# State read-out in four column groups, masked values in two row groups (HGRN sample products)

## The chip, the cores and the metric

The kernel runs on one core of a Trainium2 chip. The metric is the device time of one execution in microseconds; three runs of the kernel before gave a median of 1787.67 us (1786.09 to 1790.24). The profile is of one execution of it. Its engines are named as in the profile: PE (TensorE; PEld are its weight loads), DVE (VectorE), ACT (ScalarE), POOL (GpSimd) and SP, whose queue issues most of the DMAs.

## The reference

One decoder layer is run on 256 prompt tokens and on 32 sample tokens (8 sequences of 4). A conditioning projection (ada), one combined input projection, two mixing groups, an output projection, layer norms and a mixture of 32 experts follow each other. The change is in the first mixing group, a gated linear recurrence with 8 heads of 128 x 128 state:

```
S_t = diag(f_t) S_{t-1} + k_t v_t^T          # per head, state S of 128 x 128
o_t = S_t^T q_t
```

The reference computes it by chunks; for the samples a chunk is the 4 new tokens of a sequence:

```python
o_inter = jnp.einsum('bhtk,bhkv->bhtv', qc * jnp.exp(b), S)      # read-out of the old state
a = jnp.einsum('bhtk,bhsk,bhtsk->bhts', qc, kc, decay)
o_intra = jnp.einsum('bhts,bhsv->bhtv', a, vc)
S_new = jnp.exp(b_last)[..., None] * S + jnp.einsum(
    'bhsk,bhsv->bhkv', kc * jnp.exp(b_last[:, :, None] - b), vc)
```

Each of the 8 sample sequences has its own state per head, so per head there are 8 products of 4 tokens with a 128 x 128 state (`o_inter`), and 8 updates of 128 x 128 (`S_new`). Everything is float32.

## The kernel before

Each engine has one instruction stream written out by hand; semaphores order them. Tokens stand as columns: 256 of the prompt (`TP`) and 32 of the samples (`TS`), 288 in all (`T`). Weights arrive as 1 MB chunks in a ring of 8 slots (`ring`); SP loads the next chunk into a slot when PE has signalled `ring_used` for it. The order of PE's stream is: ada chunks and the projections of the recurrent group, then two *halves* of four heads each (L672 to L746), then the attention group, the output projection, routing and the experts.

In a half, PE alternates between dense work and the recurrence. A dense chunk (`head_chunk`, L589) is 16 matmuls of 128 x 128 weights by 288 columns, for the attention's q and k. Behind each even chunk come eight small products for the prompt's state (L708), with 32 rows each in two of the four row groups of the array and two PSUM banks. Behind each odd chunk comes one sample head:

- L718: the read-out. `qpad` holds, for each sequence b, the head's 32 query columns with all but the four of sequence b zeroed. Eight matmuls (128 rows, 32 columns, 128 moving columns) accumulate over b into the 32 partitions `32h` of bank 3, so the four heads of a half stand below one another.
- L720: the product inside the 4 new tokens (32 rows, 32 columns) is accumulated onto it, and signals `os_pe`.
- L726: the update. POOL (L497) has made `vblk`, the 32 tokens' values repeated for 8 sequences and masked with `seqmask`: 32 partitions x 1024. Two matmuls of 32 rows, 128 columns and 512 moving columns write banks 0 and 1. DVE scales the old state (L1625, after `os_pe`) and adds both banks (L1630); POOL stores the new state and loads that of the head after next.

At the start of a half PE transposes the decayed keys of its four heads: the prompt's (L686) and the samples' (L689, four transposes into 32 partitions of bank 7), which ACT copies out (L1220, L1221). At its end stand the prompt's output products (L740 and L745, the latter with 32 moving columns), and between their two pairs of heads one transpose (L734) of `osr`, DVE's copy (L1635) of the four read-outs; DVE copies the transposed result to its place (L1637). PE then waits for ACT's copy of the first pair (L1227). A whole group's value rows are projected before, with 4 partial sums for the samples that `fold_parts` (L613) adds by a matmul with `fold`, four stacked 32 x 32 identities; ACT and DVE each copy half of the 1024 columns to `tok[0:32, 5]` (L1179, L1512).

Every plain fp32 matmul shows as two records in the trace, a transpose as one.

## Time and profile before

| | |
|---|---|
| median of three runs | 1787.67 us |
| profiled execution, device time | 1787.84 us |
| its span, first to last instruction | 1786.1 us |
| PE busy | 1603.4 us (90%) |
| DVE, ACT, POOL busy | 528.3, 200.0, 94.7 us |
| mean granted TensorE clock | 0.945 |

The granted clock is given as a share of 2.4 GHz; in a stretch it reads 1.00 or 0.50. A record's duration includes its way through the array, so records of one engine overlap, and busy time is the union of them. An idle time before an instruction is given in brackets with what ended it; "issue" means that nothing the profile shows was waited for. Forms such as 128*32 are the rows and columns of the weights that a matmul uses, and 128x512 the shape that moves through them.

### The profile page before, as it was taken

The numbers are of one execution on the slowest core, as the hardware profiler recorded it, in microseconds if no ns is written. First come the engines' busy times: TensorE is split into PE (matmuls) and PEld (weight loads), VectorE is DVE, ScalarE is ACT, GpSimd is POOL, SyncE is SP. The second block draws the span as 40 slices with busy tenths as digits, with TensorE's granted clock in tenths as the row PEclk, the third lists the DMA queues.
The fourth block names the chain that finished last, engine by engine and source line by source line (L and its number), as shares of the span: only waits on it lengthen the run. The fifth ranks groups of instructions, "written<-read, shape, count | busy, mean of one in ns | idle before, by whom it ended". The sixth has DMA issues, their size and how long they took to land.

```text
span 1786.1 us, 24827 instructions
## 1 busy us (share of the span) xinstructions
PE 1603.4 (90%) x9535; PEld 913.9 (51%) x9535; DVE 528.3 (30%) x919; ACT 200.0 (11%) x335; POOL 94.7 (5%) x172
## 2 busy tenths in 40 slices
PE   3679999999999999899967999999898988999893
PEld 0036666634777775477744544454443534445351
DVE  0010009631221322542145223232323223232225
ACT  0000001300000002340025000101000000000002
POOL 3000000000110100000001000000000000000000
PEclk7679999999989989899987999999999999999997
DMA  9998888876443445184332999999999999999991
GB/s 350 422 386 333 308 333 306 328 289 237 159 129 97 151 142 186 49 314 142 141 141 107 363 407 415 401 421 421 409 411 404 412 399 411 407 414 414 414 393 61
DMA packets 79389, 536.94 MB, mean 301 GB/s; under 512 B 10385, under 2 KB 10561, under 8 KB 18065
## 3 DMA queue, kind: packets, MB, share of 16 engines
q1 hardware_dynamic: 72146, 507.62, 71.6%
q0 software_dynamic: 6576, 26.35, 4.8%
q10 hardware_dynamic: 624, 2.36, 0.3%
q8 instruction: 31, 0.51, 0.1%
q14 instruction: 12, 0.10, 0.0%
HBM read 533.40 MB, written 11.80 MB: 305 GB/s over the span
## 4 chain that ended last, share of the span: by engine, by line
PE 69%; DMA 19%; DVE 5%; SPq 4%; issue 2%; ACT 2%; ACTq 0%; DVEq 0%
PE ps L589 18%; PE ps L1095 13%; DMA ring<-w_gate 12%; PE ps L933 7%; PE ps L602 6%; PE ps L1115 5%; DMA ring<-w_ada 5%; PE ps L573 4%; SPq L383 3%; PE ps L1077 3%; DMA arena<-w_down 1%; PE ps L1041 1%; PE ps L745 1%; DVE arena L1917 1%; PE ps L1083 1%
## 5 line engine op out<-in xcount | busy, mean ns | idle before, releaser
L1095 PE MATMUL ps<-ring,arena 128*64 128x256 f32 x3200 | 359.4, 383 | 17.9 <-DMA ring<-w_gate 17.9
L589 PE MATMUL ps<-arena,ring 128*128 128x288 f32 x1280 | 321.7, 410 | 0.0
L1095 PEld LDWEIGHTS ps<-ring,arena 128*64 128x64 f32 x3200 | 227.2, 138 | 165.4 <-DMA ring<-w_gate 33.7
L589 PEld LDWEIGHTS ps<-arena,ring 128*128 128x128 f32 x1280 | 240.6, 190 | 89.8 <-issue 25.5
L1115 PE MATMUL ps<-arena 128*64 128x512 f32 x800 | 180.6, 597 | 29.7 <-DMA arena<-w_down 16.7
L573 PE MATMUL ps<-ring,silu_c 128*32 128x512 f32 x768 | 118.3, 727 | 51.2 <-DMA ring<-w_ada 24.6
L1115 PEld LDWEIGHTS ps<-arena 128*64 128x64 f32 x800 | 53.8, 136 | 140.4 <-issue 86.5
L933 PE MATMUL ps<-arena,ring 128*128 128x288 f32 x512 | 124.7, 406 | 0.0
L602 PE MATMUL ps<-ring,arena 128*128 128x512 f32 x256 | 117.2, 606 | 1.3 <-ACT arena L1179 0.7
L1077 PE MATMUL ps<-arena 64*128 64x512 f32 x384 | 104.6, 636 | 12.2 <-DVE arena L1917 10.7
L933 PEld LDWEIGHTS ps<-arena,ring 128*128 128x128 f32 x512 | 97.2, 190 | 26.8
L1933 DVE TENSOR_TENSOR arena<-arena,ps 128x256 f32<-128x256 f32 x25 | 10.5, 421 | 276.9 <-PE ps L1095 276.9
L573 PEld LDWEIGHTS ps<-ring,silu_c 128*32 128x32 f32 x768 | 20.6, 118 | 128.8 <-DMA ring<-w_ada 68.6
L602 PEld LDWEIGHTS ps<-ring,arena 128*128 128x128 f32 x256 | 47.5, 193 | 61.3 <-issue 58.1
L1077 PEld LDWEIGHTS ps<-arena 64*128 64x128 f32 x384 | 31.0, 184 | 86.8 <-issue 86.8
L1946 DVE TENSOR_TENSOR arena<-ps,arena 128x512 f32<-128x512 f32 x25 | 17.3, 691 | 164.6 <-PE ps L1115 164.6
L1917 DVE TENSOR_TENSOR arena<-arena,ps 128x1024 f32<-128x1024 f32 x48 | 58.6, 1221 | 11.3 <-PE ps L1077 8.5
L539 POOL DMA_INDIRECT arena<-u_rows,idx x26 | 29.9, 1152 | 534.3 <-PE ps L1041 533.3
L1367 ACT COPY arena<-ps 128x1024 f32<-128x1024 f32 x26 | 26.3, 1012 | 198.8 <-PE ps L1041 198.8
L1374 ACT ACTIVATE arena<-ps 128x256 f32<-128x256 f32 x25 | 9.6, 384 | 314.6 <-PE ps L1095 314.6
L1496 DVE COPY arena<-ps 128x288 f32 x8 | 3.7, 458 | 132.0 <-PE ps L589 132.0
L497 POOL TENSOR_TENSOR arena<-arena,seqmask 32x1024 f32<-32x1024 f32 x8 | 15.2, 1905 | 414.8 <-DVE arena L1512 414.7
(432 smaller groups left out, 1214.7 us busy)
## 6 DMA issues: line engine op xcount, KB each, us to landing
ring<-w_gate SPq DMA_DIRECT2D x100, 1024.0 KB, 23.9
ring<-w_up SPq DMA_DIRECT2D x100, 1024.0 KB, 26.3
arena<-w_down SPq DMA_DIRECT2D x100, 1024.0 KB, 27.0
ring<-w_ada SPq DMA_DIRECT2D x96, 1024.0 KB, 8.3
ring<-w_in SPq DMA_DIRECT2D x56, 1024.0 KB, 6.4
ring<-w_o SPq DMA_DIRECT2D x16, 1024.0 KB, 6.5
ring<-cache_k SPq DMA_DIRECT2D x16, 512.0 KB, 3.9
ring<-cache_v SPq DMA_DIRECT2D x16, 512.0 KB, 4.0
```

Source lines behind the costliest of these rows:

```text
L383: sp.dma_start(dst, src).then_inc(signal, 16)
L539: nc.gpsimd.indirect_dma_start(out=xg, out_offset=None, in_=u2_rows[:], in_offset=bass.IndirectOffsetOnAxis(idx1[:, 0:1], 0), bounds_check ...
L573: last = mm(ps[32 * j:32 * j + 32, 0, :], silu_c[:, t, :], ring[:, slot, 512 * j:512 * (j + 1)], start=(t == 0), stop=(t == KC - 1))
L589: last = mm(ps[:, bank, 0:T], ring[:, slot, P * t:P * (t + 1)], uT[:, t, :], start=(t == 0), stop=(t == KC - 1))
L602: mm(ps[:, 4 + i, :], uT[:, 4 * (c % 4) + t, t0:t0 + tn], ring[:, slot, 512 * t:512 * (t + 1)], start=(c % 4 == 0 and t == 0), stop=(c % 4 ...
L745: last = mm(o[:, CH * c4:CH * (c4 + 1)], shist[:, c - 1, h, :], hq[:, k, CH * c:CH * (c + 1)], start=False, stop=(c4 == 3))
L933: last = mm(ps[:, 4 + m % 4, 0:T], ring[:, n % SLOTS, P * k:P * (k + 1)], mixT[:, k, :], start=(k == 0), stop=(k == KC - 1))
L1077: last = mm(ps[0:tn, ((5, 6), (4, 7))[nn][r], :], spread[rows, t0:t0 + tn], yg[rows, 512 * nn:512 * (nn + 1)], start=True, stop=True, tile ...
L1095: last = mm(ps[B * s:B * (s + 1), 2 + c // 4, 0:256], xgT[:, 4 * (c % 4) + t, :], ring[:, c, 512 * t + 256 * s:512 * t + 256 * (s + 1)], s ...
L1115: last = mm(ps[B * s:B * (s + 1), 5 + nn, :], hT[:, q % 2, B * (q // 2):B * (q // 2 + 1)], mslot[q][:, 1024 * s + 512 * nn:1024 * s + 512 ...
L1367: nc.scalar.copy(xgT, ps[:, 0:2, :].rearrange("p a (m s) -> p (a m) s", s=B)).then_inc(x_copied, 1)
L1917: return v.tensor_tensor(w, w, ps[:, 5:7, :], ALU.add).then_inc(sum_dve, 1)
```

## The change

- **Read-out.** The eight matmuls of a head go to four column groups: sequence `2j + i` writes the partitions `32j`, `i` = 0, 1 accumulate there, and each head has 128 columns of bank 3 instead of 32 partitions. The product inside the new tokens is accumulated in group 0. The four partial sums are added when the result is turned: DVE copies all of bank 3 (128 x 512, into `bg2`) and four matmuls with `fold` turn and add it, in place of one transpose.
- **Masked values.** The values, the decayed keys and the mask are held twice, on partitions 0 to 31 for sequences 0 to 3 and on 32 to 63 for 4 to 7. `vblk` becomes 64 x 512, and the two matmuls of the update use row groups 0 and 1 and write banks 0 and 1. PE waits once, for all adds of the head before, and not for each bank.
- For the second copy, `fold_parts` runs twice, the four transposes of the sample keys become eight matmuls with the identity into two column groups, and ACT and DVE copy 64 partitions for 32. POOL makes `seqsel` with two small copies before it lets PE start.

```diff
+            for j in range(2):
+                link(g.tensor_copy(seqsel[32 * j:32 * j + 32, :], seqmask[:, 4 * j:4 * j + 4]))
...
-                nc.gpsimd.tensor_tensor(vblk, bc(tok[0:TS, 5, h * P:(h + 1) * P], 1, NSEQ),
-                                        bc(seqmask[:], 2, P), ALU.mult).then_inc(vblk_ready, 1)
+                nc.gpsimd.tensor_tensor(vblk, bc(tok[0:2 * TS, 5, h * P:(h + 1) * P], 1, 4),
+                                        bc(seqsel[:], 2, P), ALU.mult).then_inc(vblk_ready, 1)
...
-            def fold_parts(parts):
+            def fold_parts(parts, copies=1):
-                mm(ps[0:TS, 6, :], fold[:], parts, start=True, stop=True).then_inc(folded, 1)
+                for j in range(copies):
+                    last = mm(ps[32 * j:32 * j + 32, 6, :], fold[:], parts, start=True, stop=True)
+                last.then_inc(folded, 1)
...
                 for h in range(4):
-                    last = nc.tensor.transpose(ps[0:TS, 7, P * h:P * (h + 1)], hf[:, heads[h], TP:T], ident[:])
+                    for j in range(2):
+                        last = mm(ps[32 * j:32 * j + 32, 7, P * h:P * (h + 1)], hf[:, heads[h], TP:T], ident[:],
+                                  start=True, stop=True)
...
-                    for b in range(NSEQ):
-                        mm(ps[32 * h:32 * h + 32, 3, 0:P], qpad[:, h, b, :], s0[k % 2][:, b, :],
-                           start=(b == 0), stop=False)
-                    mm(ps[32 * h:32 * h + 32, 3, 0:P], abufs[:, k, :], tok[0:TS, 5, P * k:P * (k + 1)],
+                    for i in range(2):
+                        for j in range(4):
+                            mm(ps[32 * j:32 * j + 32, 3, P * h:P * (h + 1)], qpad[:, h, 2 * j + i, :],
+                               s0[k % 2][:, 2 * j + i, :], start=(i == 0), stop=(i == 1 and j > 0))
+                    mm(ps[0:TS, 3, P * h:P * (h + 1)], abufs[:, k, :], tok[0:TS, 5, P * k:P * (k + 1)],
                        start=False, stop=True).then_inc(os_pe, 1)
                     pe.wait_ge(vblk_ready, k + 1)
-                    for part in range(2):
-                        if k >= 1:
-                            pe.wait_ge(us_dve, 3 * k - 1 + part)
-                        mm(ps[:, part, :], kdts[:, h, :],
-                           vblk[:, 4 * part:4 * part + 4, :].rearrange("p b v -> p (b v)"), start=True, stop=True
-                           ).then_inc(us_pe, 1)
+                    if k >= 1:
+                        pe.wait_ge(us_dve, 3 * k)
+                    for j in range(2):
+                        mm(ps[:, j, :], kdts[32 * j:32 * j + 32, h, :],
+                           vblk[32 * j:32 * j + 32].rearrange("p b v -> p (b v)"), start=True, stop=True,
+                           tile_position=(32 * j, 0)).then_inc(us_pe, 1)
...
-                        nc.tensor.transpose(ps[:, 3, P:2 * P], osr, ident[:]).then_inc(osr_pe, 1)
+                        for h in range(4):
+                            last = mm(ps[:, 3, TS * h:TS * (h + 1)], osr[:, P * h:P * (h + 1)], fold[:],
+                                      start=True, stop=True)
+                        last.then_inc(osr_pe, 1)
...
-                v.tensor_copy(osr, ps[:, 3, 0:P]).then_inc(osr_dve, 1)
+                v.tensor_copy(osr, ps[:, 3, :]).then_inc(osr_dve, 1)
```

PE's stream keeps its order. From the last chunk of the first half to the end of its sample head it read (names in brackets are the semaphores waited for):

```order
L589 MATMUL ps<-arena,ring 128x288 x15
L718 MATMUL ps<-arena 32x128 [waits s0_loaded1]
L718 MATMUL ps<-arena 32x128 x7
L720 MATMUL ps<-arena 32x128
L726 MATMUL ps<-arena 128x512 [waits us_dve,vblk_ready]
L726 MATMUL ps<-arena 128x512 [waits us_dve]
```

Now it reads, with the projection as L592, the read-out L726, the product inside the tokens L728 and the update L734:

```order
L592 MATMUL ps<-arena,ring 128x288 x15
L726 MATMUL ps<-arena 32x128 [waits s0_loaded1]
L726 MATMUL ps<-arena 32x128 x7
L728 MATMUL ps<-arena 32x128
L734 MATMUL ps<-arena 128x512 [waits us_dve,vblk_ready]
L734 MATMUL ps<-arena 128x512
```

The counts are the same; one wait is gone, and the groups of the array that the matmuls use (which don't show here) differ. From the middle of the first half's output products to the first chunk of the second half PE's stream was:

```order
L745 MATMUL ps<-arena 128x32 x4
L734 MATMUL ps<-ident,arena 128x128 [waits osr_dve]
L740 MATMUL ps<-arena 128x128 [waits hgo_act]
L745 MATMUL ps<-arena 128x32 x3
...
L686 MATMUL ps<-ident,arena 128x128 x7
L689 MATMUL ps<-ident,arena 32x128 x4
L589 MATMUL ps<-arena,ring 128x288 [waits evac_act,slot_loaded0]
```

and is now (output products L751 and L756, fold L743, prompt transposes L691, sample keys L695):

```order
L756 MATMUL ps<-arena 128x32 x4
L743 MATMUL ps<-fold,bg 128x32 [waits osr_dve]
L743 MATMUL ps<-fold,bg 128x32 x3
L751 MATMUL ps<-arena 128x128 [waits hgo_act]
L756 MATMUL ps<-arena 128x32 x3
...
L691 MATMUL ps<-ident,arena 128x128 x7
L695 MATMUL ps<-ident,arena 32x128 x8
L592 MATMUL ps<-arena,ring 128x288 [waits evac_act,slot_loaded0]
```

One transpose has become four matmuls ahead of the wait for ACT, and four transposes eight matmuls ahead of the first chunk.

## Rows read from the trace of the kernel before

**Rows 1.** The page: busy tenths of PE in 40 slices of the span.

```profile
PE   3679999999999999899967999999898988999893
```

**Rows 2.** Stretches: PE, PEld, DVE, ACT, POOL busy (instructions), PEclk, DMA share, GB/s.

```profile
436.00:523.40 87.40, 87.40 (x437) 64.61 (x436) 24.39 (x41) 3.07 (x6) 13.75 (x11) 1.00 0.43 140
523.50:540.50 17.00, 15.82 (x71) 14.90 (x71) 0.91 (x9) 1.87 (x3) 3.60 (x4) 0.50 0.30 78
540.60:625.80 85.20, 85.20 (x420) 62.57 (x418) 22.04 (x32) 2.27 (x6) 10.30 (x8) 1.00 0.39 130
625.90:642.90 17.00, 16.59 (x79) 16.20 (x79) 1.51 (x2) 1.17 (x2) 1.64 (x3) 0.50 0.16 47
```

**Rows 3.** Waits of SP's queue, 430 to 1000 us: total us, times, longest.

```profile
SPq L335 <- PE ps L589: 102.3, 11, 11.5
SPq L394 <- DVE plan L1875: 10.9, 1, 10.9
```

**Rows 4.** Timeline, first sample head, PE: start us, us, what [idle before].

```profile
454.09 1.94 PE L718 MATMUL ps<-arena 128*32 128x128 f32 x16
455.95 0.40 PE L720 MATMUL ps<-arena 32*32 32x128 f32 x2
456.28 1.98 PE L726 MATMUL ps<-arena 32*128 32x512 f32 x4
458.19 8.03 PE L589 MATMUL ps<-arena,ring 128*128 128x288 f32 x32
```

**Rows 5.** Timeline: rotating column groups (L809), alternating row groups (L708, L1077).

```profile
759.39 1.93 PE L809 MATMUL ps<-ring,arena 128*32 128x128 f32 x64
...
445.04 1.16 PE L708 MATMUL ps<-arena 32*128 32x128 f32 x16
...
1378.33 2.10 PE L1077 MATMUL ps<-arena 64*128 64x512 f32 x8
```

**Rows 6.** Timeline: transposes of the sample keys, first and second half.

```profile
436.75 0.60 PE L689 MATMUL ps<-ident,arena 128*32 128x128 f32 x4
...
538.70 1.06 PE L689 MATMUL ps<-ident,arena 128*32 128x128 f32 x4
```

**Rows 7.** Timeline: the second value fold and DVE's copies around it.

```profile
433.25 0.69 DVE L1508 COPY arena<-ps 128x512 f32<-128x512 f32 x1 [7.37 <-PE ps L607]
434.00 1.05 PE L613 MATMUL ps<-arena,fold 128*32 128x512 f32 x2 [0.81 <-DVE arena L1508]
435.08 0.68 DVE L1512 COPY arena<-ps 32x512 f32<-32x512 f32 x1
```

**Rows 8.** Timeline: end of the first half, around the read-out's transpose.

```profile
522.25 0.28 DVE L1635 COPY arena<-ps 128x128 f32<-128x128 f32 x1
...
525.88 1.75 PE L745 MATMUL ps<-arena 128*128 128x32 f32 x8
527.45 0.45 PE L734 MATMUL ps<-ident,arena 128*128 128x128 f32 x1
527.67 0.58 ACT L1227 COPY arena<-ps 128x512 f32<-128x512 f32 x1 [18.80 <-PE ps L745]
528.31 0.80 PE L740 MATMUL ps<-arena 128*128 128x128 f32 x2 [0.41 <-ACT arena L1227]
```

**Rows 9.** Timeline: start of the program on POOL and PE.

```profile
15.83 0.93 POOL L478 COPY fold<-ident 32x32 f32<-32x32 f32 x4
18.91 4.40 PE L573 MATMUL ps<-ring,silu_c 128*32 128x512 f32 x24 [18.91 <-POOLq L486]
22.25 0.16 PEld L573 LDWEIGHTS ps<-ring,silu_c 128*32 128x32 f32 x8 [1.43 <-DMA ring<-w_ada]
```

**Rows 10.** Timeline of the key transposes after the halves; stretches around them.

```profile
639.32 4.58 PE L759 MATMUL ps<-ident,arena 128*128 128x128 f32 x24
639.20:642.90 3.70, 3.70 (x19) 3.61 (x19) 1.22 (x1) 0.59 (x1) 0.01 (x1) 0.50 0.00 0
643.00:646.00 3.00, 3.00 (x14) 1.73 (x13) 2.34 (x2) 0.00 (x0) 1.34 (x3) 1.00 0.57 228
```

More of the change, by code:

```diff
@@ L76, in layer @@
         fold = sb("fold", [P, TS])
+        seqsel = sb("seqsel", [2 * TS, 4])
         silu_c = sb("silu_c", [P, KC, 32])
@@ L148, in layer @@
         shist = area(TMP, 8, 4, P)
-        kdts = area(TMP + 4096, 4, P, parts=TS)
+        kdts = area(TMP + 4096, 4, P, parts=2 * TS)
         abuf = area(TMP + 4608, 2, H, P)
@@ L154, in layer @@
         kdt = area(TMP + 7040, 2, 4, P)
-        osr = area(TMP + 8064, P)
-        vblk = area(TMP + 8192, NSEQ, P, parts=TS)
+        osr = bg2[:]
+        vblk = area(TMP + 8192, 4, P, parts=2 * TS)
         s0 = [area(TOK + 1024 * i, NSEQ, P) for i in range(2)]
@@ L657, in _ @@
                     pe.wait_ge(parts_act, 1)
-                    fold_parts(parts_hi)
+                    fold_parts(parts_hi, 2)
                     pe.wait_ge(evac_act, 15)
@@ L671, in _ @@
             pe.wait_ge(parts_dve, 1)
-            fold_parts(parts_hi)
+            fold_parts(parts_hi, 2)
             pe.wait_ge(evac_dve, 15)
@@ L1178, in evacuate_rows @@
                 act.wait_ge(folded, n_fold)
-                nc.scalar.copy(tok[0:TS, slot + 2, 0:512], ps[0:TS, 6, :]).then_inc(evac_act, 1)
+                nc.scalar.copy(tok[0:2 * TS, slot + 2, 0:512], ps[0:2 * TS, 6, :]).then_inc(evac_act, 1)
             act.wait_ge(lb_dve, 1)
@@ L1220, in _ @@
                 nc.scalar.copy(kdt, ps[:, 0:2, :].rearrange("p a (h s) -> p a h s", s=P))
-                nc.scalar.copy(kdts, ps[0:TS, 7, :].rearrange("p (h s) -> p h s", s=P)).then_inc(kd_act, 1)
+                nc.scalar.copy(kdts, ps[0:2 * TS, 7, :].rearrange("p (h s) -> p h s", s=P)).then_inc(kd_act, 1)
                 for c in range(0, SLOTS, 2):
@@ L1511, in evacuate_rows @@
                 dve.wait_ge(folded, n_fold)
-                v.tensor_copy(tok[0:TS, slot + 2, 512:1024], ps[0:TS, 6, :]).then_inc(evac_dve, 1)
+                v.tensor_copy(tok[0:2 * TS, slot + 2, 512:1024], ps[0:2 * TS, 6, :]).then_inc(evac_dve, 1)
             N_G = N_MIX + 2 * MIX + 2
@@ L1634, in _ @@
                     dve.wait_ge(osr_pe, 1)
-                v.tensor_copy(osr, ps[:, 3, 0:P]).then_inc(osr_dve, 1)
+                v.tensor_copy(osr, ps[:, 3, :]).then_inc(osr_dve, 1)
                 dve.wait_ge(osr_pe, half + 1)
-                v.tensor_copy(hout[:, heads, TP:T], ps[:, 3, P:2 * P].rearrange("p (h t) -> p h t", t=TS)
+                v.tensor_copy(hout[:, heads, TP:T], ps[:, 3, 0:P].rearrange("p (h t) -> p h t", t=TS)
                               ).then_inc(osm_dve, 1)
```

## The prediction

> **What bounds the kernel now.** I read the slices of the span first: PE reads 8 or 9 tenths in most slices [rows 1]. The change touches one stage, the recurrent head group from about 436 to 643 us, so the stretches of that stage come next [rows 2]. From 436 to 523.4 us PE is busy 87.40 of 87.40 us at a granted clock of 1.00 (the 2.4 GHz level) with the DMA engines at 0.43. From 523.5 to 540.5 and from 625.9 to 642.9 us the clock reads 0.50 (1.2 GHz) and PE is still busy 15.82 and 16.59 of 17 us. So PE's own stream sets the pace here, at either level. The waits of the DMA queue say the same from the other side: SP waited 102.3 us in total for PE to free ring slots before it could load more w_in [rows 3], so weights lie ready.
>
> A microsecond taken from PE in this stage should therefore arrive at the end of the span if nothing later is pinned to an absolute time. The expert loads are the only place where DMA bounds later, and SP waited 10.9 us there for the routing plan [rows 3], which comes out of the PE, DVE and ACT chain. The loads start earlier when the plan does.
>
> Inside the stage the timeline of one sample head [rows 4] shows what stands between two dense projection chunks: 16 records of the state read-out (each fp32 matmul is two records) in 1.94 us, two of the intra-sample product, then four records of the masked-value product in 1.98 us. From the first read-out record at 454.09 to the next chunk at 458.19 are 4.10 us, eight times in all.
>
> **Read-out in four column groups.** Now all 16 records of a head write the same 32 partitions, one after the other: a record lasts 0.27 us, so the step is (1.94 - 0.27) / 15 = 0.111 us. The value product of the attention later has the same shape (128 rows by 32 columns, 128 moving columns) and rotates over four column groups: 64 records in 1.93 us [rows 5], so one round of four takes the step of one record here. Sixteen records in four rounds take 0.27 + 3 x 0.111 = 0.60 us. Saved: 1.94 - 0.60 = 1.34 us a head, 10.7 us over eight heads. Ends: 0 if nothing overlaps, 10.7 if all does. I take 10.7, as the row has the same shape and the same rotation.
>
> **Masked values in two row groups.** The four records step at (1.98 - 0.59) / 3 = 0.46 us. Two row groups with a bank each exist already: the prompt's state update runs 16 records of 32 rows in 1.16 us where the 16 of the read-out need 1.94, and the expert combine runs 8 records of 64 rows by 512 columns in 2.10 us [rows 5]. By the first, a pair takes 0.06 x 2 = 0.12 us against 0.111 for one; by the second, a round of two steps (2.10 - 0.64) / 3 = 0.49 us. Two rounds: 0.61 + 0.49 = 1.10 us. Saved 0.88 us a head, 7.0 us over eight (ends: 0 and 7.3, the latter with a step of 0.46). The two separate waits of before become one on the adds of the previous head, two dense chunks back; behind it in PE's queue stands the next chunk, and the adds wait for nothing but PE. GpSimd's masking instruction has half the elements a partition, so the state stores queued behind it don't get later.
>
> **The doubled transposes.** Four transposes a half (one record each) become eight matmuls against the identity (16 records) in two column groups: eight rounds for four. At the high level a step is (0.60 - 0.27) / 3 = 0.11 us, at the low one (1.06 - 0.42) / 3 = 0.21 us [rows 6], and the second half starts at the low level. Added: 4 x 0.11 + 4 x 0.21 = 1.3 us on PE's path (ends: 0 at no extra rounds, 3.8 if the groups don't overlap and twelve records are added). ACT's copy of 64 instead of 32 partitions is the same length: DVE's 32x512 copy takes 0.68 us, its 128x512 copy 0.69 [rows 7].
>
> **The fold products.** One transpose a half becomes four matmuls, 8 records of 128 by 128 weights with 32 moving columns, the shape of the inter-chunk product before it: 8 records in 1.75 us at the low level [rows 8], that is 0.21 each, 1.7 us to the next start. Now PE goes from the transpose (527.45) to the next product (528.31) in 0.86 us, of which most is the wait for ACT's copy [rows 8]. So 0.84 us comes on the path a half, 1.7 in all (ends: about 0 at the high level, where ACT's copy hides it, and 1.7).
>
> In front of it DVE copies 128x512 where it copied 128x128: 0.69 for 0.28 us [rows 7, 8]. The copy starts at 522.25, PE wants it at 527.45: hidden by 5 us of products, and 0.41 us a half if that cover were gone. The Trainium skill (TensorEngine Tiling (Array Packing), PSUM Bottleneck) warns that tiling speeds up the matmuls and not the emptying of PSUM, so that the copy can become the bound. By that rule the copy would cost up to 0.8 us over both halves; the rows leave 4.5 us of slack and I take 0.
>
> **The two value folds of the projection** run twice into two column groups. Two records take 1.05 us [rows 7]; two more in another group run beside them, 0 taken, 0.9 us over both calls if they don't.
>
> **Two small mask copies** are added on GpSimd before it lets PE start. Four such copies take 0.93 us [rows 9], two 0.5. PE starts at 18.91 behind GpSimd but is out of loaded weights at 22.25 [rows 9], so the delay is swallowed: 0, or 0.5 us.
>
> **Sum:** -10.7 - 7.0 + 1.3 + 1.7 = -14.7 us. The profiled execution took 1787.84 us (span 1786.1 and 1.7 around it), 0.2 above the median of 1787.67. 1787.84 - 14.7 = 1773.1 us.
>
> **The clock.** Both low stretches begin shortly after PE reaches the narrow products at the end of a half and end after the transposes that follow. At half level PE takes twice as long per step (0.21 for 0.11), so a low stretch longer or shorter by x us moves the end by x / 2. The new blocks are shorter and denser, the fold products are more of the narrow kind; I take no net effect and keep 4 us either way, which is also the spread of the three runs (1786.09 to 1790.24). The Trainium skill (TensorE: Matmul & The Clock Gate, Part 4) says that PE transposes don't count as activity for the clock. By that rule the identity matmuls that replace transposes would bring the second half back to the high level sooner, at most 0.9 us. The trace speaks against it: from 639.2 to 642.9 PE does nothing but transposes at 0.50, and reads 1.00 from 643.0 on [rows 10]. I take 0.
>
> **Rivals.**
> Overlap of neighbours only. Both records of a matmul go to the same column group one behind the other; if PE starts them strictly in order, the second record of one overlaps only the first of the next. The read-out would take 9 steps for 16 (0.78 us saved), the masked product 3 for 4 (0.46): 9.9 us saved, the transposes would cost 1.6, the folds 1.7 and 0.9, in all -5.7: 1782. Against it: 64 records in 1.93 us are four abreast [rows 5].
> Column groups only. The masked product signals after each of its two matmuls, and the rows of two groups in [rows 5] may signal once. If that holds the pair apart, 7.0 us are not won: 1780. For it there is no row; against it, two matmuls into two banks share nothing.
> Given back later. A later stage is set by a transfer and swallows the gain: 1787.5. Against it the waits of SP [rows 3].
> Slower. The sparser activity between chunks drops the clock inside a half, over dense chunks. A stretch of 17 us at 0.50 costs up to 8.5 us of dense work. It decides from 1.7 such stretches on; with two the kernel takes 1773.1 + 17 = 1790. Against it: before, the eight blocks were twice as long, and within the halves the clock read 1.00 throughout [rows 2].
>
> **Chances.** Forecast 80%, neighbours only 7%, column groups only 5%, given back 4%, slower 4%. A difference of 0.2% (3.6 us) is about what can be told from none. Below 1784.1 lie the first three: 92%, of which I move 2 to no change for the terms not bounded by a row. Faster 0.90, same 0.05, slower 0.05. The range goes down by the fold at the high level (1.7) and some 3.4 us of clock to 1768, and up to 1781.5, which takes in the second rival and ends half a microsecond short of the first.
>
> **What would show it.** In the changed profile: a read-out of 16 records in about 0.60 us and a masked product in about 1.1 us, so 2.0 us less between chunks eight times; 16 identity records in about 0.9 and 1.7 us; 8 fold records of 1.7 us a half with no wait for DVE; two low stretches of about 17 us at the ends of the halves and none inside; the routing plan and the first expert block some 14 us earlier. The prediction is wrong if a read-out block takes 1 us or more, if the clock reads 0.50 inside a half, or if the plan comes earlier and the end doesn't.

## The result and the profile after

The changed kernel took 1752.23, 1757.92 and 1760.06 us, the middle one the median (one further run of 6512 us was disturbed and counts in nothing here), the kernel before 1786.09 to 1790.24 us beside it. The ratio is 0.9824, with an interval of [0.9808, 0.9839]: some 31 us faster, about twice the 14.7 us of the forecast, and below the range that ended at 1768.0. The profiled execution of it is the fastest, 1752.23 us (span 1750.5). A later comparison gave 1757.63 us (1755.13 to 1761.97, five runs) and 0.9827 [0.9809, 0.9845].

PE stays the busiest engine; the slices of the page answer to [rows 1], the same view before the change:

```profile
PE   3679999999999999899967999999989989889893
```

The stretches of the recurrent stage answer to [rows 2], cut where the granted clock changes (us, PE, PEld, DVE, ACT, POOL busy with instructions, PEclk, DMA share, GB/s):

```profile
435.00:512.90 77.90, 77.90 (x433) 56.83 (x433) 20.79 (x38) 3.08 (x6) 9.63 (x10) 1.00 0.41 146
512.90:518.40 5.50, 5.50 (x52) 5.50 (x50) 3.31 (x8) 0.58 (x1) 0.93 (x1) 1.00 0.65 265
518.40:532.00 13.60, 12.84 (x62) 11.28 (x62) 0.53 (x7) 2.07 (x3) 2.69 (x3) 0.50 0.20 59
532.00:606.70 74.70, 74.70 (x405) 54.23 (x404) 19.15 (x29) 1.59 (x4) 7.73 (x8) 1.00 0.41 136
606.70:622.40 15.70, 15.19 (x114) 12.93 (x113) 6.80 (x8) 1.17 (x2) 3.29 (x5) 1.00 0.44 179
```

The reader is to see two things. The heads before the first output product take 77.90 us for some 85.7. And of the two low stretches of 17 us one has become 13.6 us and begins 5.5 us behind the first output product; the other, at the end of the second half, is gone in this profile.

The first sample head on PE answers to [rows 4] (read-out, product inside the tokens, masked product, next chunk):

```profile
454.02 0.64 PE L726 MATMUL ps<-arena 128*32 128x128 f32 x16
454.59 0.40 PE L728 MATMUL ps<-arena 32*32 32x128 f32 x2
454.92 1.13 PE L734 MATMUL ps<-arena 32*128 32x512 f32 x4
455.98 0.75 PE L592 MATMUL ps<-arena,ring 128*128 128x288 f32 x2
```

From 454.02 to 455.98 are 1.96 us where 4.10 stood. The doubled keys of both halves answer to [rows 6]:

```profile
436.02 1.07 PE L695 MATMUL ps<-ident,arena 128*32 128x128 f32 x16
...
527.83 1.92 PE L695 MATMUL ps<-ident,arena 128*32 128x128 f32 x16
```

The second value fold and DVE's copy of it answer to [rows 7]; four records take the 1.05 us that two took:

```profile
433.16 1.05 PE L617 MATMUL ps<-arena,fold 128*32 128x512 f32 x4 [0.81 <-DVE arena L1519]
434.26 0.68 DVE L1523 COPY arena<-ps 64x512 f32<-64x512 f32 x1
```

The end of the second half, at the high level, answers to [rows 8]: DVE's copy of the read-out, the last products of the first pair, the fold products, ACT's copy, the second pair.

```profile
609.06 0.68 DVE L1646 COPY bg<-ps 128x512 f32<-128x512 f32 x1
...
609.92 0.98 PE L756 MATMUL ps<-arena 128*128 128x32 f32 x8
...
610.73 1.06 PE L743 MATMUL ps<-fold,bg 128*128 128x32 f32 x8
610.93 0.58 ACT L1238 COPY arena<-ps 128x512 f32<-128x512 f32 x1 [14.75 <-PE ps L756]
611.60 0.30 PEld L751 LDWEIGHTS ps<-arena 128*128 128x128 f32 x2
611.62 0.47 PE L751 MATMUL ps<-arena 128*128 128x128 f32 x2
```

The fold products run without a wait, and 0.89 us after their start the second pair starts; before it was 0.86 from the transpose to there. In the first half they stand at the high level too, from 516.92 to 517.82 us. SP's waits answer to [rows 3], the mask copies and PE's start to [rows 9], the key transposes behind the halves, at the high level in this profile, to [rows 10]:

```profile
SPq L336 <- PE ps L592: 94.5, 11, 11.4
...
SPq L395 <- DVE plan L1886: 10.7, 1, 10.7
```

```profile
15.83 0.42 POOL L478 COPY seqsel<-seqmask 32x4 f32<-32x4 f32 x2
16.31 0.93 POOL L481 COPY fold<-ident 32x32 f32<-32x32 f32 x4
...
19.39 3.64 PE L576 MATMUL ps<-ring,silu_c 128*32 128x512 f32 x16 [19.39 <-POOLq L489]
...
615.65 1.94 PE L770 MATMUL ps<-ident,arena 128*128 128x128 f32 x16
```

To see where the rest came from I cut every profile at the same instructions: *heads* from the first key transpose to the first output product, and in the second half from its first dense chunk; *ends* from the first output product to the next half's first chunk or the attention's first transposes of cached keys; *experts* from the first expert product to the first product behind the last block. All in us, from one profiled execution each; "fall" is the time from the first output product to the fall of the granted clock to 0.50, first half / second half.

| kernel | heads | ends | of it at 0.50 | fall | experts |
|---|---|---|---|---|---|
| before | 170.5 | 40.8 | 33.1 | 2.0 / 1.5 | 772.3 |
| before, again | 171.5 | 41.6 | 34.7 | 1.2 / 2.4 | 773.5 |
| after | 154.9 | 32.5 | 11.3 | 5.5 / none | 766.7 |
| after, again | 154.2 | 33.0 | 12.7 | 10.5 / 6.5 | 765.9 |
| x1 read-out only | 160.8 | 27.5 | 1.2 | 10.6 / none | 774.2 |
| x2 masked values only | 164.0 | 32.9 | 13.6 | 7.3 / 7.2 | 764.9 |
| x3 before + added work | 171.5 | 44.0 | 36.5 | 1.3 / 1.5 | 774.3 |
| x4 after + dense filler | 169.5 | 36.4 | 20.5 | 5.8 / 4.8 | 765.9 |
| x5 before + dense at the ends | 175.6 | 32.4 | 14.2 | 6.8 / 7.2 | 773.6 |
| x6 after + 8 narrow products | 157.5 | 27.6 | 0 | none / none | 765.1 |
| y2 after + a copy of the old block | 161.8 | 39.0 | 26.3 | 6.6 / 2.8 | 769.3 |

Before to after, the two first profiles: heads -15.6, ends -8.3, experts -5.6; the attention's score and value products 50.2 to 45.2, -5.0; all other stages -1.1; together -35.6, the difference of the spans. The -5.0 is an accident of the execution: both programs show 48.4 there in their second profile, where the rest is heads -17.3, ends -8.6, experts -7.6. So three things have to be explained: the work of the heads (forecast), the ends of the halves, and the experts, which the change doesn't touch.

### The profile page after: what moved, and what is told of

It reads as the page before. It is cut to its first block, busy times and chain, and to the rows that moved or that the text cites. A ratio compares the mean times of both kernels' runs of the same rounds, so it can differ in the third digit from the quotient of the medians.

```text
span 1750.5 us, 24913 instructions
## 1 busy us (share of the span) xinstructions
PE 1570.4 (90%) x9577; PEld 891.4 (51%) x9577; DVE 527.8 (30%) x919; ACT 200.1 (11%) x335; POOL 88.2 (5%) x174
## 4 chain that ended last, share of the span: by engine, by line
PE 68%; DMA 18%; DVE 5%; SPq 4%; issue 2%; ACT 2%; ACTq 0%; DVEq 0%
PE ps L592 18%; DMA ring<-w_gate 14%; PE ps L1106 13%; PE ps L944 7%; PE ps L605 6%; PE ps L1126 6%; DMA ring<-w_ada 5%; PE ps L576 4%; SPq L384 3%; PE ps L1088 3%; PE ps L1052 1%; DVE arena L1928 1%; PE ps L796 1%; PE ps L610 1%; PE ps L1094 1%
## 5 line engine op out<-in xcount | busy, mean ns | idle before, releaser
L592 PE MATMUL ps<-arena,ring 128*128 128x288 f32 x1280 | 322.2, 411 | 0.0
L592 PEld LDWEIGHTS ps<-arena,ring 128*128 128x128 f32 x1280 | 241.1, 191 | 89.6 <-issue 25.6
L1088 PE MATMUL ps<-arena 64*128 64x512 f32 x384 | 104.6, 636 | 12.3 <-DVE arena L1928 10.7
L1944 DVE TENSOR_TENSOR arena<-arena,ps 128x256 f32<-128x256 f32 x25 | 10.5, 421 | 277.4 <-PE ps L1106 277.4
L1957 DVE TENSOR_TENSOR arena<-ps,arena 128x512 f32<-128x512 f32 x25 | 17.3, 692 | 158.4 <-PE ps L1126 158.4
L1928 DVE TENSOR_TENSOR arena<-arena,ps 128x1024 f32<-128x1024 f32 x48 | 58.6, 1221 | 11.3 <-PE ps L1088 8.5
L1378 ACT COPY arena<-ps 128x1024 f32<-128x1024 f32 x26 | 26.3, 1012 | 198.3 <-PE ps L1052 198.3
L1388 ACT COPY arena<-ps 128x512 f32<-128x512 f32 x25 | 14.6, 585 | 188.2 <-PE ps L1126 188.2
```

The source lines that it names most:

```text
L592: last = mm(ps[:, bank, 0:T], ring[:, slot, P * t:P * (t + 1)], uT[:, t, :], start=(t == 0), stop=(t == KC - 1))
L1088: last = mm(ps[0:tn, ((5, 6), (4, 7))[nn][r], :], spread[rows, t0:t0 + tn], yg[rows, 512 * nn:512 * (nn + 1)], start=True, stop=True, tile ...
L1378: nc.scalar.copy(xgT, ps[:, 0:2, :].rearrange("p a (m s) -> p (a m) s", s=B)).then_inc(x_copied, 1)
L1928: return v.tensor_tensor(w, w, ps[:, 5:7, :], ALU.add).then_inc(sum_dve, 1)
```

## The experiments

### Which part gives what

**x1**, the kernel before with the read-out in four column groups and its fold products alone, shown here; **x2**, the masked values, keys and mask on two row groups alone (the change with x1's edit undone).

```diff
- mm(ps[32 * h:32 * h + 32, 3, 0:P], qpad[:, h, b, :], s0[k % 2][:, b, :],
+ mm(ps[32 * j:32 * j + 32, 3, P * h:P * (h + 1)], qpad[:, h, 2 * j + i, :],
...
- nc.tensor.transpose(ps[:, 3, P:2 * P], osr, ident[:]).then_inc(osr_pe, 1)
+ last = mm(ps[:, 3, TS * h:TS * (h + 1)], osr[:, P * h:P * (h + 1)], fold[:],
```

> The kernel before with the read-out in four column groups and the fold product alone; masked values and sample keys as before. The changed kernel gained some 30 us where the work on TensorE explains 15; the rest is less time at the low clock (the second half's low stretch is gone, that of the attention is shorter). By work alone: read-out -8 x 1.3 = -10.4, fold 0 to +1.7, so 9 to 10.5 us under the kernel before. Theory A, sparse activity (the narrow blocks pull the clock down at the ends of the halves, and fewer narrow records pull less): 9 to 10.5 and at least 5 more from the clock, 15 or more under it. Theory B, chance (where a low stretch falls is an accident of each program): 10 give or take 4, the runs' clocks scattering about that of before. Theory C, matmuls in place of transposes hold the clock up: like A, with the clock gain at the second half's end, since the fold is here.

> The kernel before with the masked values in two row groups alone (with the doubled sample keys and value folds); read-out and its transpose as before. By work alone: -8 x 0.86 = -6.9, doubled transposes +0.4 to +1.3: 5.6 to 6.5 us under the kernel before. Theory A (sparse activity): that and some 3 to 8 us from the clock. Theory B (chance): 6 give or take 4. Theory C (matmuls for transposes): a gain of clock at the starts of the halves, where the identity matmuls are.

x1: 1770.21 us (1762.33 to 1778.95), 0.9911 [0.9886, 0.9936]. x2: 1768.35 us (1765.86 to 1771.84), 0.9896 [0.9882, 0.9911]. Alone, the parts win 17.6 and some 19 us, together more than the 31 of both. The table says why: heads -9.7 and -6.5 add up to about the change's, but the profiles show that each part alone already takes the early fall of the clock away, which can be won once. x1 fits theory A (15 us or more) and theory C as well, which x3 tests. x2 won more than A had for it (8.6 to 14.5 us): its experts are short too, x1's are not. Six runs of x1 lie in two groups, 1762 to 1765 us at a mean clock of 0.955 to 0.957 and 1775 to 1779 us at 0.949 to 0.951. The profile is of the first group; that the second had longer low stretches is what the mean clock suggests, and no profile shows where.

x1's ends: 10.6 us at 1.00 behind the first output product, then 3.4 at 0.50, and the second end wholly at 1.00.

```profile
516.80:527.40 10.60, 9.83 (x88) 9.73 (x88) 3.03 (x13) 1.17 (x2) 4.48 (x4) 1.00 0.55 167
527.40:530.80 3.40, 3.40 (x13) 2.57 (x12) 0.00 (x0) 1.48 (x2) 0.00 (x0) 0.50 0.24 78
608.90:624.60 15.70, 15.19 (x113) 12.94 (x113) 5.95 (x8) 1.17 (x2) 3.29 (x5) 1.00 0.45 158
```

### Does the added work hold the clock up?

**x3**, the kernel before with the identity matmuls in place of the sample key transposes and narrow products in place of the read-out's transpose, no more.

```diff
- last = nc.tensor.transpose(ps[0:TS, 7, P*h:P*(h+1)], hf[:, heads[h], TP:T], ident[:])
+ for j in range(2): last = mm(ps[32*j:32*j+32, 7, P*h:P*(h+1)], hf[:, heads[h], TP:T], ident[:], ...)
```

> The kernel before with only the change's added matmuls: eight identity matmuls for four transposes of the sample keys, four narrow matmuls for the transpose of the read-out; read-out and update as slow as before. By work: +1.3 for the sample keys, 0 to +1.7 for the narrow ones: 1 to 3 us over the kernel before. Theories A and B: that, with low stretches at the ends of both halves as before. Theory C (matmuls where transposes were hold the clock up): 5 us or more under the kernel before, the second half's low stretch gone.

1790.76 us (1777.92 to 1796.64, twelve runs), 0.9996 [0.9971, 1.002]. In its profile the early falls are all there, at 1.3 and 1.5 us. Inconclusive all the same: four of the twelve runs took 1778 to 1780 us at a mean clock of 0.958 to 0.959, the other eight 1786 to 1797 us at 0.945 to 0.950, and no profile shows what was different in the four. This work may help in some executions; it doesn't do what the change does in all of them.

### What stands between the heads and the output products

**x4**, the change with four dense products (128 x 128 by 288 columns, result unused) behind each masked product; **x5**, the kernel before with the same four behind the last head of each half only; **x6**, the change with eight narrow products (32 columns out, unused) there.

```diff
+ for t in range(4): mm(ps[:, 7, 0:T], ident[:], uT[:, t, :], ...)             # x4, x5
...
+ for t in range(8): mm(ps[0:TS, 7, 0:P], uT[:, t, TP:T], ident[:], ...)       # x6
```

> The changed kernel with four dense matmuls (128 x 128 weights, 288 columns, results unused) behind each sample head, 8 records of 0.243 us, some 2.1 us with their drain, so that a head takes about as long as before, 17 us in all. Theory A (sparse activity): the clock gain stays, 17 us over the changed kernel, about 1775, no low stretch at the second half's end. If it is the length of a head, or the moment at which the ends of the halves fall, that decides: the low stretches are back and the time is that of the kernel before, 1788 to 1790. Theory B (chance): anything between 1775 and 1792, by where the stretches fall.

> The kernel before with four dense matmuls (128 x 128 weights, 288 columns, results unused) only behind the last sample head of each half, in front of the output products: some 2.1 us twice, 4.2 us of added work. Theory A (the sparse head in front of the narrow output products pulls the clock down early, 1.5 to 2.0 us after the first of them in the profile before): the clock falls later at the ends of both halves, the low stretches there are shorter than 17 us, and the kernel is no slower than before: 1780 to 1788. Theory B (chance) and theory C (matmuls for transposes): the stretches at the ends stay at about 17 us, 1787.8 + 4.2 = 1792.

> The changed kernel with eight matmuls into one column group (128 rows, 32 columns, 128 moving columns, results unused) only behind the last sample head of each half: 16 records in 1.94 us as the read-out of before, 3.9 us of added work. Theory A: the clock falls early again at the ends of both halves, within 2 to 3 us of the first output product, and stays low for some 14 to 17 us: 1757.9 + 3.9 + 5 to 12 = 1767 to 1774. Theories B and C: 1757.9 + 3.9 = 1762, stretches as in the changed kernel.

x4: 1776.23 us (1766.02 to 1777.96), 0.9925 [0.9905, 0.9945]. The time is the one forecast with theory A, but its profile has a low stretch at the second half's end, which A there had excluded: the falls come at 5.8 and 4.8 us, and 20.5 us are at 0.50. With heads about as long as before (169.5 us) the fall stays late, so the pace of the heads alone doesn't bring it early. What stands right ahead of the output products is dense work here, as in x5. x5: 1785.64 us (1781.97 to 1787.13), 0.9979 [0.9969, 0.9989]: 2.0 us of dense work at each end put the fall off to 6.8 and 7.2 us and shorten the ends from 40.8 to 32.4 us, which pays for the 4 to 5 us longer heads and leaves some 3 us:

```profile
524.10:530.90 6.80, 6.27 (x56) 6.08 (x55) 2.52 (x9) 0.58 (x1) 3.48 (x3) 1.00 0.54 131
530.90:541.20 10.30, 9.53 (x39) 8.32 (x39) 0.12 (x1) 2.06 (x3) 0.09 (x1) 0.50 0.13 42
626.10:633.30 7.20, 6.67 (x60) 6.48 (x58) 0.29 (x1) 0.58 (x1) 1.09 (x2) 1.00 0.39 112
```

x6: 1760.83 us (1752.42 to 1765.32), 0.9847 [0.983, 0.9864], no fall in its profile. Theory A had forecast an early fall and 1767 to 1774 us, and missed: 1.9 us of narrow work behind the fast block isn't enough to bring the early fall back.

**y2** therefore put all of the old block there: eight narrow products and two masked products over 32 rows, results unused, behind the last head of each half; the signal of that head's update to DVE moves behind them.

```diff
+ for t in range(8): mm(ps[0:TS, 7, 0:P], uT[:, t, TP:T], ident[:], ...)
+ for j in range(2): mm(ps[:, 7, :], kdts[0:TS, h, :], vblk[0:TS]..., ...).then_inc(us_pe, 1)
```

> The changed kernel with a copy of the old head block behind the last head of each half: 8 products into 32 columns and 2 products over 32 rows with 512 columns moving, results unused, some 3.7 us each time. Theory A (4 us of work on a part of the array right before the output products bring the early fall of the clock): the clock falls within 2.5 us of the first output product at both ends, the ends measure 18 to 20 and 21 to 23 us without the copy's own 3.7 us, and the time is 1758 + 7.4 + 8 = 1773 us. Rival (the copy's place alone, without what surrounded it before, does nothing to the clock): no fall within 4.8 us of it, time 1758 + 7.4 = 1765 us.

1773.72 us (1768.04 to 1776.41), 0.9923 [0.9905, 0.9941], the time of theory A, but the early fall in one half only. The block takes its 3.8 us; the fall comes 2.8 us behind the first output product in the second half, and 6.6 us in the first. Some 3 us of the time are of another kind: the experts take 769.3 us, with 13.2 us of idle time on PE for which the profile shows no wait, where x4 has 9.9. So the hit of the time is partly luck. The lines are the block, and the stretches around both first output products (517.93 and 613.9):

```profile
514.16 1.94 PE L741 MATMUL ps<-ident,arena 128*32 128x128 f32 x16
516.02 1.98 PE L743 MATMUL ps<-arena 32*128 32x512 f32 x4
517.93 0.49 PE L759 MATMUL ps<-arena 128*128 128x128 f32 x2
```

```profile
517.90:524.50 6.60, 6.60 (x60) 6.57 (x59) 2.72 (x8) 0.59 (x1) 2.63 (x4) 1.00 0.26 83
524.50:534.80 10.30, 9.53 (x49) 8.29 (x49) 1.19 (x5) 1.56 (x3) 0.99 (x1) 0.50 0.25 74
613.90:616.70 2.80, 2.80 (x27) 2.80 (x26) 1.29 (x2) 0.00 (x0) 1.39 (x2) 1.00 0.00 0
616.70:633.80 17.10, 17.10 (x82) 16.56 (x82) 2.74 (x3) 1.17 (x2) 1.02 (x3) 0.50 0.16 65
```

What is shown: with the old block of 4.1 us right ahead of the output products the clock fell within 3 us in both halves of all nine profiles that have it (the two of before, x3 and the six below that only move memory); without it, or with dense work between, not before 4.8 us, or not at all, in 16 ends (the change twice, x1, x2, x4 to x6, and x8 below); with the old block put behind the new one, in one of two. x5 adds nothing to the kernel before but dense work at that place, and puts the fall off. What of the block the chip answers to was not told apart.

### The two kernels again

> The changed kernel itself, once more, for a second profile and more times. If the clock's stretches belong to the program (A, C): again a short or no low stretch at the second half's end, median 1755 to 1762. If they are accidents of a run (B): stretches at the ends of halves of any length, times scattered from 1752 up to 1773, where the work alone would put it.

> The kernel before itself, for a second profile. A and C: low stretches of some 17 us at the ends of both halves again, beginning within 3 us of the first output product. B: other places or lengths; the stage of the experts, which the change doesn't touch, shows what differs between two profiles of one program.

1757.63 us for the change and 1788.39 us for one run of before: the second profiles of the table. The experts' difference stays, the attention's doesn't. At the ends the change has 12.7 us at 0.50 for 11.3, but in other places: 3.4 us in the first half and, against theory A's letter, 10.2 us in the second, where the first profile had none. What the change keeps is the late fall, not a half without one.

### Why the experts got faster

The programs whose experts take some 766 us are those that hold `seqsel` (after, x2, x4, x6; y2 holds it too, and takes 3 us more for the idle time named there). Its 16 bytes per partition take up 32 behind `fold`, and every later tensor lies 32 bytes higher: the arena, into which `w_down` is loaded, at byte 101888 instead of 101856. **x7** is the kernel before with an unused tensor of the same size; **x8** the change with `seqsel` declared behind the arena.

```diff
         fold = sb("fold", [P, TS])
+        pad = sb("pad", [2 * TS, 4])            # x7, from before
-        seqsel = sb("seqsel", [2 * TS, 4])      # x8, from after
...
         arena = sb("arena", [P, ARENA])
+        seqsel = sb("seqsel", [2 * TS, 4])      # x8
```

> The kernel before with one unused tensor of 32 bytes per partition put behind `fold`, where the change has `seqsel`; no instruction differs, but every later tensor of the on-chip memory lies 32 bytes higher, the arena at byte 101888 instead of 101856. Theory L (the 7 to 8 us of the stage of experts come from where the tensors lie): the stage falls from some 773.5 to some 766 us and the time to 1780 to 1781 us; the ends of the halves stay at 39 to 43 us. Rival M (they come from the different work in the attention before it, by the clock or by the order of the transfers): stage 773 to 774 us, time 1788 us as before.

> The changed kernel with `seqsel` declared behind the arena, so that the arena and all before it lie where they lay in the kernel before; the instructions are those of the change. Theory L: the stage of experts is back at some 773.5 us and the time 7 to 8 us over the changed kernel's, 1765 to 1767 us. Rival M: stage 766 us, time 1757 to 1759 us.

x7: 1781.91 us (1779.02 to 1782.61), 0.9962 [0.9949, 0.9974], experts 766.6 us, ends 40.1. x8: 1764.84 us (1758.64 to 1767.28), 0.9869 [0.985, 0.9889], experts 773.4 us. Both as the theory of the layout has it. What is shorter on PE is a wait. The line is the down projection, its busy time, the mean of one and the idle time ahead of it with what ended it, of the kernel before and of x7, whose instructions are the same:

```profile
L1115 PE MATMUL ps<-arena 128*64 128x512 f32 x800 | 180.6, 597 | 29.7 <-DMA arena<-w_down 16.7 <-DVE arena L1935 12.9
```

```profile
L1116 PE MATMUL ps<-arena 128*64 128x512 f32 x800 | 180.2, 597 | 22.0 <-DVE arena L1936 12.9 <-DMA arena<-w_down 9.1
```

And the loads themselves run faster. The lines are what the DMA engines moved from 980 to 1700 us, of the kernel before and of x7, whose first expert products start at 988.8 and 988.7 us. x7 moved 0.75% more in the same time; 0.75% of 772 us are, as an estimate, 5.8 us, for the 5.6 that its experts are shorter:

```profile
DMA packets 41532, 292.86 MB, mean 407 GB/s; under 512 B 5851, under 2 KB 5851, under 8 KB 5979
```

```profile
DMA packets 41835, 295.07 MB, mean 410 GB/s; under 512 B 5885, under 2 KB 5885, under 8 KB 6013
```

**x11** moves the arena alone, by 32 bytes; **x9** and **x10** move everything behind `fold` by 96 and 64; **x12** and **x13** the arena alone by 160 and 288. All are the kernel before with one pad, as x7's, behind `fold` or ahead of the arena.

> The kernel before with a pad of 32 bytes directly ahead of the arena: the arena at byte 101888, every other tensor of the attention where it was. Theory D (what counts is where the transfers into the arena land, above all `w_down`): as the pad behind `fold`, stage of experts some 766.6 us, time 1780 to 1782 us. Rival (another tensor's place counts): 773 us and 1787 us.

> The kernel before with a pad of 96 bytes behind `fold`: the arena at byte 101952, a multiple of 64 and not of 128 or more. Theory D with a boundary of 64 bytes: time 1780 to 1782 us, stage of experts some 766.6 us. If a coarser boundary (128 or 512 bytes) counts: 1787 us, stage 773 us.

> The kernel before with a pad of 64 bytes behind `fold`: the arena at byte 101920, 32 bytes past a multiple of 64, as in the kernel before. Theory D with a boundary of 64 bytes: 1787 us and stage 773 us, as before. If any move helps (distance, not boundary): 1780 to 1782 us.

> The kernel before with a pad of 160 bytes directly ahead of the arena: the arena at byte 102016, a multiple of 128 and not of 256. If a boundary of 128 bytes counts: 1780 to 1782 us, stage of experts some 766.5 us; if a coarser one: 1787 to 1789 us, stage 772 to 773 us.

> The kernel before with a pad of 288 bytes directly ahead of the arena: the arena at byte 102144, a multiple of 256 and not of 512. If a boundary of 128 or 256 bytes counts: 1780 to 1782 us, stage of experts some 766.5 us; if one of 512 bytes or this address alone: 1787 to 1789 us, stage 772 to 773 us.

| kernel | arena at byte | past a multiple of 256 | time, ratio | experts | wait for `w_down` |
|---|---|---|---|---|---|
| before | 101856 | 224 | 1788 | 772.3 | 16.7 |
| x11 | 101888 | 0 | 1781.47, 0.9959 [0.9945, 0.9973] | 766.2 | 8.9 |
| x10 | 101920 | 32 | 1788.96, 1.0003 [0.9995, 1.0012] | 772.8 | 17.2 |
| x9 | 101952 | 64 | 1788.37, 0.9999 [0.9987, 1.001] | 771.6 | 16.3 |
| x12 | 102016 | 128 | 1789.05, 0.9998 [0.9989, 1.0006] | 773.3 | 17.0 |
| x13 | 102144 | 0 | 1778.95, 0.994 [0.9927, 0.9953] | 766.7 | 7.0 |

My boundary of 64 bytes fell with x9, one of 128 with x12; 256 fits all. (The profile of x13 is of a run of 1786.0 us, which lost time ahead of the experts; its other four runs took 1777.8 to 1779.3.) The lines of x12 and x13:

```profile
L1116 PE MATMUL ps<-arena 128*64 128x512 f32 x800 | 180.8, 597 | 29.9 <-DMA arena<-w_down 17.0 <-DVE arena L1936 12.9
```

```profile
L1116 PE MATMUL ps<-arena 128*64 128x512 f32 x800 | 180.2, 597 | 20.0 <-DVE arena L1936 12.9 <-DMA arena<-w_down 7.0
```

The Trainium skill (DMA: Bandwidth & Descriptors, How a descriptor splits into AXI transactions) says, by the vendor's account, that a transfer is cut into transactions of 256 bytes and that each must start at a multiple of 256; it tells it of reads. By that a row of 8192 bytes that starts off such a multiple would take 33 for 32, which on the third of the expert bytes that goes to the arena gives, as an estimate, 1/32 x 1/3 x 772 = 8 us. The trace agrees in size, with 5.6 to 7.6 us. For the ring, with two thirds of the bytes, the same estimate is 16 us, and y3 below measured half of that. By the same section of the Trainium skill an offset of 64 should cost less than one of 224; here x9 costs what the kernel before does.

### Two versions that beat both

**y1** puts the eighth chunk of each half between its two pairs of output products, on top of the change. **y3** is y1 with the weight ring, at byte 16512 (128 past a multiple of 256), moved to 16640 and the arena to 102144, by a pad of 128 bytes ahead of each. The small tensors behind the ring move with it. The diff is y1's.

```diff
                     if pair == 1:
+                        pe.wait_ge(slot_loaded[7], loaded(N_SQ + 8 * half + 7))
+                        pe.wait_ge(evac_dve, 18 + 4 * half)
+                        head_chunk(7, 5)
                         pe.wait_ge(osr_dve, half + 1)
...
                 v.tensor_copy(osr, ps[:, 3, :]).then_inc(osr_dve, 1)
+                evacuate_head(projT[:, 8 * half + 7, :], N_SQ + 8 * half + 7, 5)
```

> The changed kernel with the eighth weight chunk of each half placed between its two pairs of output products (VectorE's copy of that chunk behind the copy of the read-out). 32 products of 288 columns, 8 us, then stand where TensorE now waits for VectorE and where the clock falls in some runs. Theory A: no fall at the ends; stages heads and end together shrink by the waits there and the low clock, 2 to 6 us, time 1752 to 1756 us. Rival: slot 7 of the weight ring is freed some 8 us later, its next load lands late, and what is won is waited for in the chunks behind: 1757 to 1760 us.

> The kernel of y1 with a pad of 128 bytes ahead of the weight ring and one of 128 bytes ahead of the arena: the ring at byte 16640 instead of 16512, the arena at 102144, both multiples of 256. If the place of the destination counts by 256 bytes for every load: the ring takes twice the bytes of `w_down`, so up to twice its 7 us come off the stage of experts (766.9 to some 753 us), 1 to 2 us off the first stage, and the time is 1733 to 1742 us. If the arena alone is special: stage 766 us, time 1749 to 1752 us as y1.

y1: 1749.93 us (1749.42 to 1752.28), 0.9793 [0.9778, 0.9807], the least spread of all, and below its forecast of 1752 to 1756. Both halves with their ends take 182.3 us for the change's 187.4. Its first end, with the chunk in the middle, stays at 1.00 for 17 us, and 3.4 us are left at 0.50, where the forecast had no fall:

```profile
505.08 0.49 PE L755 MATMUL ps<-arena 128*128 128x128 f32 x2
...
509.12 8.01 PE L592 MATMUL ps<-arena,ring 128*128 128x288 f32 x32
516.96 0.97 PE L747 MATMUL ps<-fold,bg 128*128 128x32 f32 x8
```

```profile
505.10:522.10 17.00, 16.85 (x114) 15.06 (x112) 5.42 (x16) 0.69 (x2) 3.62 (x4) 1.00 0.54 178
522.10:525.50 3.40, 2.78 (x18) 2.36 (x20) 0.00 (x0) 0.48 (x1) 0.00 (x0) 0.50 0.01 5
```

y3: 1743.13 us (1742.06 to 1755.92), 0.9758 [0.9734, 0.9782], just above its forecast of 1733 to 1742. The experts take 759.4 for 766.9 us, and the first dense chunk starts at 110.8 for 112.8: the place counts for the ring too, with half of what I had put at most. From 1020 to 1680 us the DMA engines moved 276.67 MB for y1's 273.48. PE's wait for `w_down` is all but gone. Its wait for `w_gate` stays, with 21.8 us (y1: 21.4), so the loads still hold PE up:

```profile
L1112 PE MATMUL ps<-ring,arena 128*64 128x256 f32 x3200 | 360.6, 384 | 21.9 <-DMA ring<-w_gate 21.8
...
L1132 PE MATMUL ps<-arena 128*64 128x512 f32 x800 | 178.6, 596 | 13.7 <-DVE arena L1953 12.9 <-DMA arena<-w_down 0.4
```

## Why the prediction was wrong in its size

**What bounds the kernel: right.** What PE won arrived at the end. SP still waits 94.5 us for PE's slots, and about as long as before (10.7 us) for the plan. The first expert product starts at 958.5 for 988.8 us.

**Read-out and masked values: right.** 0.64 for the forecast 0.60 us, 1.13 for about 1.1; a head block 1.96 for 2.0. Eight times 4.10 - 1.96 are 17.1 us for the forecast 17.7. The first and second rival fell with these rows.

**Doubled transposes: right.** 1.07 and 1.92 us, 0.47 and 0.86 more than in [rows 6], for 0.44 and 0.85. Value folds, mask copies and DVE's wider copy cost nothing on the path, as taken: the copy ends at 609.74, the fold products start at 610.73.

**Fold products: mis-sized.** The sum has 0.84 us a half, at the low level. They ran at the high level, and ACT's copy covers them: 0.89 for 0.86 us. This was the lower end that the working named. In x3's profile, where they run at the low level, they take 1.70 us from 529.04 us on, as the working had it. With the lower end the work is -17.1 + 1.3 + 0.1 = -15.7 us. Of this, 1.0 us (the second half's doubled transposes, the fold products) stands in the ends, so the rows give -16.7 for the heads, which measure -15.6 and -17.3. The low clock explains the two: it reaches 1.0 us into the heads of the second half before and 2.4 after in the first pair of profiles, 2.9 and 1.0 in the second. With half of each difference taken off, by the forecast's own x / 2, both come to -16.3.

**The clock: the step that failed.** "I take no net effect and keep 4 us either way." It was 8.3 to 8.6 us at the ends, all in the direction of faster: before, 33.1 and 34.7 us stood at 0.50 there, after it 11.3 and 12.7. I read where the low stretches begin and end, and not what PE had done just before them; in every profile of the kernel before, the old block of the last head stood there. The forecast that two low stretches of about 17 us remain at the ends was wrong in both halves of both profiles. That none appears inside a half held, and the slower rival fell with it.

**The experts: no term at all.** 5.6 to 7.6 us came from a 32-byte tensor that moved the destination of a stream of loads. The sum went over instructions only; the order of a program doesn't show addresses. The rival that a transfer might swallow the gain was looked at, that a transfer might get faster was not.

Of the some 31 us between the two kernels, some 16 are thus the work of the heads, about 8.5 the ends, by the clock, and about 7 the place of the arena. The mechanism that the forecast summed is right and gives about half of the gain; the rest came from two places that it had put at nothing. Open stay what in the old block brings the clock down, what the four shorter runs of x3 had, and why a given end falls in one execution and not in the next.

## What to carry to other kernels

Compare the addresses of large DMA destinations before and after a change that adds or drops a tensor, even one of 32 bytes, and put buffers that take streams of loads at a multiple of 256 bytes. Where low stretches of the clock begin at one place of the program in every execution, ask what stands just ahead of that place and whether the change touches it; independent dense work moved there, as in y1, was worth some 6 us here (0.9793 for 0.9827). When stages that a change doesn't touch get faster, test for the layout with a pad before looking for a mechanism.

## What was new about the hardware

- Loads of 1 MB into SBUF (rows of 8192 bytes) got slower when the destination was 32, 64, 128 or 224 bytes past a multiple of 256, by about the same each time: 5 to 8 us of some 773 us in which a third of the bytes went there. Aligning the ring, with two thirds of them, gave 7.5 us of 766.9.
- Two value-fold matmuls in two column groups (four records) took 1.05 us, as one (two records) did; sixteen records in four column groups took 0.64 for 1.94.
- 4.1 us of products on a part of the array right ahead of narrow products went with a fall of the clock within 3 us, with PE busy throughout, in 18 of 18 ends, but in one of two when it stood behind a faster block; 2 us of dense products between the two put it off to 6.8 and 7.2 us.
